# Attention on one core: rests of the turned weights in one bank for two groups, value products over 128 rows and then over 64

## The chip, the cores and the metric

The kernel runs on one core of one Trainium2 chip. The metric is the device time of one execution in microseconds; before the change the median of three runs is 2397.38 (2395.8 to 2399.34).

## The reference, cut to what matters

The reference is a trunk of two layers over 1024 tokens with 1024 features. Layer 0 mixes with a short convolution and a recurrence, layer 1 with sliding-window attention; each is followed by a squared-ReLU MLP. The change touches the attention alone:

```
scores = einsum("bcqkgd,bcskd->bckgqs", q, k_band) * HEAD_DIM ** -0.5   # 64-token chunks
scores = where(valid, scores + bias, NEG_INF)          # own chunk and the one before: band of 128 keys
m = maximum(max(scores), sink)
p = exp(scores - m)
denom = sum(p) + exp(sink - m)
o = einsum("bckgqs,bcskd->bcqkgd", p / denom, v_band)  # 16 query heads, 2 key/value heads, head_dim 64
y = o @ w_o
```

## The kernel before, in words

The attention works on eight tiles of 128 queries. The 16 heads of a tile go in four groups of four; groups 0 and 1 belong to the first key/value head, 2 and 3 to the second. A tile of 128 queries sees a window of WIN = 192 keys, so the weights of a group are 128 x 768 numbers. V is token-major in `VTOK`, nine blocks of 128 keys offset by 64 (`v_transposes`, `v_tokens_dve`); GpSimd copies the two blocks of a tile to `VST` (`v_tile`).

The loop is a software pipeline written out by hand (`attention`, and one function per engine: `round_pe`, `round_dve`, `round_act`, `round_pool`). A round works on the scores of tile `new` and on the values of tile `old = new - 1`. Six of the rounds (new = 2 to 7) have both; four of these are in a hardware loop. Each engine runs its queue in order and waits on semaphores; a `Track` numbers the steps of a tile.

- TensorE: per group g, `score_products` of group g + 1 (two fp32 products of 384 columns; the last of the round is group 0 of the next tile), then `probs_transposes` of group g of the old tile: four transposes of 128 x 128 into bank 4 (the block "a", the first 128 keys), four of 128 x 64 into the lower rows of bank 5 (the "rest", the last 64 keys). Groups 1 to 3 wait until both copies of the group before have emptied the banks. Behind group 3 come the `value_products`.
- VectorE: per group the biases (four operations), the maximum, the negation (`scores_dve`). Behind group 0 also the reciprocal of the old tile's denominators and the scaling of its group 0. It copies the rests out of bank 5 into `PTB` (`rest_copy`), one copy per group.
- ScalarE: per group four exponentials with their sums, then the copy of block "a" out of bank 4 into `PTA`. At the end of the round it copies the outputs of banks 6 and 7 into `Q`.
- GpSimd: scales the weights of groups 1 to 3 of the old tile, copies queries and V blocks.

`value_products` makes eight products: for each key/value head (bank 6, bank 7) one over `PTA` and one over `PTB`, each for even and odd heads (`par`), which go to the lower and upper 64 rows of the bank. All have 128 contracted rows and 512 columns. `PTB` holds only 64 rows of weights; its other 64 are set to zero once (`ptb_zero`) and contracted with what V has there. An fp32 product stands in the trace as two records.

## Time and profile before

| | |
|---|---|
| median of the runs, us | 2397.38 |
| profiled execution, its own time, us | 2398.16 |
| its span, us | 2396.4 |
| granted clock of TensorE, mean | 0.992 |
| TensorE busy, us | 2322.3 |
| VectorE busy, us | 1440.1 |
| ScalarE busy, us | 795.2 |
| GpSimd busy, us | 411.2 |
| attention, first value product to the end of the last, us | 1523.66 to 1635.95 |

The profiled execution is one run; its span is the time between the first and the last instruction, and the rest of its own time lies around it. Rows of the trace give a start in us from the span's start, a length, and the line of the kernel. PE is TensorE's products, PEld its weight loads, DVE VectorE, ACT ScalarE, POOL GpSimd.

### The profile page before, as it was taken

The page shows a single profiled execution, that of the slowest core. Times are in us where ns is not written, and L with a number is a line of the kernel's source. Part 1 is how long each engine was busy: PE and PEld are TensorE (multiplying, and loading weights), DVE is VectorE, ACT ScalarE, POOL GpSimd, SP SyncE. Part 2 cuts the span into 40 slices and gives each one's busy share as a digit, 9 for nine tenths or more (in the row PEclk, how much of TensorE's full clock was granted, in tenths as well). Part 3 has the DMA queues.
Part 4 walks back from the last instruction along what each step waited for, and adds up shares of the span by engine and source line. Part 5 has one row for each costly group of instructions (what it writes and reads, how often), then busy time and mean ns, then how long its engine had stood idle before and what let it go on. Part 6 is the DMA issues. An engine that isn't in the chain of part 4 may idle for free.

```text
span 2396.4 us, 41386 instructions
## 1 busy us (share of the span) xinstructions
PE 2322.3 (97%) x16368; PEld 1897.3 (79%) x16368; DVE 1440.1 (60%) x1994; ACT 795.2 (33%) x1265; POOL 411.2 (17%) x401
## 2 busy tenths in 40 slices
PE   7999999999999999999999999788999999999999
PEld 6888877787788888888888788446888888888887
DVE  4444567776347656655765823873465576567655
ACT  5111235444233322332333422563243233323323
POOL 0000011121232111211111400432321111111110
PEclk9999989999999999999999999999999999999999
DMA  3231100002111121111111110001111111121113
GB/s 127 71 140 58 45 11 4 3 3 100 53 43 55 44 62 53 44 53 53 53 50 54 48 53 27 1 0 40 40 53 53 53 53 44 52 61 44 53 53 88
DMA packets 167185, 119.30 MB, mean 50 GB/s; under 512 B 3662, under 2 KB 164260, under 8 KB 166564
## 3 DMA queue, kind: packets, MB, share of 16 engines
q1 hardware_dynamic: 164284, 100.65, 14.2%
q0 software_dynamic: 2736, 17.04, 1.9%
q8 instruction: 86, 1.41, 0.3%
q14 instruction: 23, 0.19, 0.0%
q10 hardware_dynamic: 56, 0.01, 0.0%
HBM read 106.68 MB, written 10.49 MB: 49 GB/s over the span
## 4 chain that ended last, share of the span: by engine, by line
PE 93%; DVE 4%; issue 1%; ACT 1%; DMA 0%; SPq 0%; DVEq 0%; ACTq 0%
PE ps L280 35%; PE ps L404 25%; PE ps L397 15%; PE ps L1189 2%; PE ps L1211 1%; PE ps L1962 1%; PE ps L2314 1%; DVE probs L1991 1%; PE ps L296 1%; PE ps L351 1%; DVE softmax_stats L1996 1%; PE ps L1248 1%; PE ps L1931 1%; PE ps L1726 1%; PE ps L1387 1%
## 5 line engine op out<-in xcount | busy, mean ns | idle before, releaser
L235 ACT CAST w_hi<-w_raw 128x1024 fp32r<-128x1024 f32 x180 | 189.3, 1052 | 813.6 <-PE ps L280 594.1
L764 DVE TENSOR_TENSOR residual<-residual,ps 128x512 f32<-128x512 f32 x448 | 299.6, 686 | 159.6 <-PE ps L404 155.8
L280 PE MATMUL ps<-h_hi,w_hi 128*128 128x512 f32 x1232 | 383.1, 392 | 4.8 <-DVE h_lo L647 3.7
L280 PE MATMUL ps<-h_lo,w_hi 128*128 128x512 f32 x1232 | 379.9, 389 | 0.0
L280 PE MATMUL ps<-h_hi,w_lo 128*128 128x512 f32 x1232 | 379.3, 389 | 0.0
L280 PEld LDWEIGHTS ps<-h_hi,w_hi 128*128 128x128 f32 x1232 | 229.2, 188 | 52.9 <-issue 4.5
L280 PEld LDWEIGHTS ps<-h_hi,w_lo 128*128 128x128 f32 x1232 | 231.3, 188 | 48.6
L280 PEld LDWEIGHTS ps<-h_lo,w_hi 128*128 128x128 f32 x1232 | 231.3, 188 | 48.6
L239 DVE TENSOR_TENSOR w_lo<-w_raw,w_hi 128x1024 fp32r<-128x1024 f32 x180 | 224.6, 1248 | 26.8 <-ACT w_hi L235 26.8
L732 POOL TENSOR_TENSOR w_sums_raw<-w_raw 128x256 f32<-128x256 f32 x64 | 52.0, 813 | 1067.3 <-DMA w_raw<-in_mlp_down 647.6
L397 PE MATMUL ps<-h_hi,w_hi 128*128 128x512 f32 x512 | 199.2, 389 | 0.0
L397 PE MATMUL ps<-h_lo,w_hi 128*128 128x512 f32 x512 | 199.2, 389 | 0.0
L397 PE MATMUL ps<-h_hi,w_lo 128*128 128x512 f32 x512 | 199.2, 389 | 0.0
L746 DVE SCALAR_TENSOR_TENSOR stage<-ps,rms_inverse 128x1024 f32<-128x1024 f32 x32 | 39.2, 1225 | 212.5 <-PE ps L280 212.5
L404 PE MATMUL ps<-t_hi,w_sums_hi 128*128 128x512 f32 x384 | 149.7, 390 | 0.0
L404 PE MATMUL ps<-t_hi,w_sums_lo 128*128 128x512 f32 x384 | 149.4, 389 | 0.0
L404 PE MATMUL ps<-t_lo,w_sums_hi 128*128 128x512 f32 x384 | 149.4, 389 | 0.0
L665 ACT CAST w_sums_hi<-w_sums_raw 128x1024 fp32r<-128x1024 f32 x64 | 67.2, 1049 | 227.9 <-POOL w_sums_raw L738 227.9
L397 PEld LDWEIGHTS ps<-h_lo,w_hi 128*128 128x128 f32 x512 | 96.1, 188 | 19.9
L397 PEld LDWEIGHTS ps<-h_hi,w_lo 128*128 128x128 f32 x512 | 96.1, 188 | 19.9
L397 PEld LDWEIGHTS ps<-h_hi,w_hi 128*128 128x128 f32 x512 | 96.1, 188 | 19.9
L642 DVE TENSOR_TENSOR stage<-ps,rms_inverse 128x1024 f32<-128x1024 f32 x30 | 36.7, 1225 | 110.3 <-PE ps L280 98.2
(389 smaller groups left out, 4012.9 us busy)
## 6 DMA issues: line engine op xcount, KB each, us to landing
w_raw<-in_mlp_up SPq DMA_DIRECT2D x64, 512.0 KB, 4.1
w_raw<-in_mlp_down SPq DMA_DIRECT2D x64, 512.0 KB, 3.4
w_raw<-in_w_in_ab SPq DMA_DIRECT2D x26, 512.0 KB, 3.8
w_raw<-in_w_qkv SPq DMA_DIRECT2D x10, 512.0 KB, 3.9
x_in_tile<-in_x POOLq DMA_DIRECT2D x8, 512.0 KB, 7.3
x_spill<-residual POOLq DMA_DIRECT2D x1, 4096.0 KB, 12.6
w_raw<-in_w_out_ab SPq DMA_DIRECT2D x8, 512.0 KB, 3.9
w_raw<-in_w_o SPq DMA_DIRECT2D x8, 512.0 KB, 3.9
```

What stands on the lines that cost most here:

```text
L235: nc.scalar.copy(WH[:, slot], WR[:, slot]).then_inc(w_hi, 1)
L239: nc.vector.tensor_tensor(WL[:, slot], WR[:, slot], WH[:, slot].bitcast(F32), ALU.subtract).then_inc(w_lo, 1)
L280: m = nc.tensor.matmul(acc(a_slot, half), ww, xx[:, k, half * HALF:(half + 1) * HALF], start=first, stop=last)
L296: m = nc.tensor.matmul(acc(1, half), ww, xx[:, k, half * HALF:(half + 1) * HALF], start=first, stop=last)
L397: m = nc.tensor.matmul(acc(slot, half), ww, xx[:, k, half * HALF:(half + 1) * HALF], start=first, stop=last)
L404: m = nc.tensor.matmul(PS[:, bank_n, :], ww[:, c], xx[:, c], start=new and c == 0 and ww is wh and xx is bh, stop=c == 1 and ww is wl, ski ...
L642: nc.vector.tensor_tensor(dst, acc2(slot), RI[:, :], ALU.mult).then_inc(acc_free[slot], 1)
L665: nc.scalar.copy(WSH[:, d % 2], WSR[:, d % 2]).then_inc(s_hi, 1)
L732: TT(raw[:, 0], a21, a22, ALU.add).then_inc(w_sum, 1)
L746: return nc.vector.scalar_tensor_tensor(dst, src, 0.0, scale, ALU.max, ALU.mult)
L764: dn_dve.done(TT(xk, xk, PS[:, bank_n, :], ALU.add), step)
L1189: m = MM(block_bank(bank_n, 32)[quarter(q), h], left[quarter(q), h], right[quarter(q), h], start=True, stop=True)
```

## The change

The nine offset blocks of V become eight plain ones, `VTOK` (the first 128 keys of each tile's window), and `VREST`, which holds for each tile the last 64 keys of the window twice, in the lower and in the upper 64 partitions. TensorE turns the latter with 16 operations of half width, ScalarE copies them (`v_rest_act`) before its first group of tile 1.

The weights' rests of groups 0 and 1 (and of 2 and 3) go into the lower and the upper rows of bank 5: the lower by a transpose, the upper by a true product with the identity (`turned`). ScalarE copies both at once into `PTB` ("r0", "r1"), behind the copy of the odd group's block "a". VectorE's rest copies go. Block "a" turns through banks 4, 6, 7 and 4 (`TA_BANK`).

`value_products` now goes by group: four pairs over 128 rows with 256 columns, the groups to banks 6, 7, 6, 7; then eight products over 64 rows (lower half of rows to bank 6, upper half to bank 7), 256 columns each. Only the first product of each bank and half of rows has `start`, and each of the last four products counts one step. ScalarE's output copies take the new order of heads in the banks. In the last round VectorE's split of the first output weights moves ahead.

```diff
--- before.py
+++ after.py
@@ -164,10 +164,11 @@
     SQ = at("squares", [S], 198.5)
     QST = at("q_tile", [2, KD, P], 32)
     VST = at("v_window", [2, 2, P], 43)
-    VTOK = at("v_token_major", [9, P], 190.5)
+    VTOK = at("v_token_major", [NT, P], 190.5)
+    VREST = at("v_rest_twice", [NT, P], 198.5)
     PP = at("probs", [2, NQ, WIN], 50)
     PTA = at("probs_t_a", [NQ, P], 74)
-    PTB = at("probs_t_b", [NQ, P], 82)
+    PTB = at("probs_t_b", [NKV, 4, P], 82)
     STA = at("softmax_stats", [2, 6, NQ], 195.25)
     QF = at("first_q_tile", [KD, P], 112)
     PF = (at("first_probs0", [4, WIN], 180.5), at("first_probs1", [4, WIN], 183.5), at("first_probs2", [4, WIN], 104))
@@ -1755,12 +1756,22 @@
 
             unit(9, 1, 4, {2: scores(0), 3: lambda: mean_square(8, 0), 4: scores(1), 6: spread_and_scores})
 
+        def turned(dst, src, half):
+
+            if half:
+                return nc.tensor.matmul(dst, src, ident, start=True, stop=True)
+            return nc.tensor.transpose(dst, src, ident)
+
         def v_transposes(t):
             t.wait_ge(acc_free[1], STAGE["qkv"][1] // 2 + 6)
             t.wait_ge(qk_norm, 2 + 9)
             sc_dve.wait(t, 0, "b3")
-            for n in range(9):
-                m = nc.tensor.transpose(bank((6, 7, 5)[n // 4])[:, n % 4], VP[:, P * n:P * n + P], ident)
+            for n in range(NT):
+                m = nc.tensor.transpose(bank(6 + n // 4)[:, n % 4], VP[:, P * n:P * n + P], ident)
+            m.then_inc(v_tr, 1)
+            for n in range(NT):
+                for half in two:
+                    m = turned(bank(4 + n // 4)[half_rows(half), n % 4], VP[:, P * n + P:P * n + P + RH], half)
             m.then_inc(v_tr, 1)
 
         def qkv_act(act):
@@ -1851,20 +1862,26 @@
 
         def v_tokens_dve(dve):
             dve.wait_ge(v_tr, 1)
-            for n in (0, 1, 2):
-                rows = 4 if n < 2 else 1
-                nc.vector.tensor_copy(VTOK[:, 4 * n:4 * n + rows], bank((6, 7, 5)[n])[:, 0:rows]).then_inc(v_tok, 1)
+            for n in two:
+                nc.vector.tensor_copy(VTOK[:, 4 * n:4 * n + 4], bank(6 + n)).then_inc(v_tok, 1)
+
+        v_rest = sem("v_rest_token_major")
+
+        def v_rest_act(act):
+            act.wait_ge(v_tr, 2)
+            for n in two:
+                nc.scalar.copy(VREST[:, 4 * n:4 * n + 4], bank(4 + n)).then_inc(v_rest, 1)
 
         q_pool = Track("q_tile_copied", ["q"])
-        v_pool = Track("v_tile_copied", ["v"])
+        v_pool = Track("v_tile_copied", ["own", "rest"])
         p_pool = Track("probs_pool", ["p1", "p2", "p3"])
         sc_pe = Track("score_pe", [f"sc{g}" for g in range(4)])
-        pv_pe = Track("value_pe", [f"t{w}{g}" for g in range(4) for w in "ab"] + ["pv"])
+        pv_pe = Track("value_pe", [f"t{w}{g}" for g in range(4) for w in "ab"] + ["pv0", "pv1", "pv2", "pv3"])
         sc_dve = Track("score_dve", [f"{w}{g}" for g in range(4) for w in ("b", "max", "neg")] + ["sink"])
-        pv_dve = Track("value_dve", ["den", "rcp", "p0", "e0", "e1", "e2", "e3"])
+        pv_dve = Track("value_dve", ["den", "rcp", "p0"])
         sc_act = Track("score_act", [f"e{g}" for g in range(4)] + ["sink"])
-        pv_act = Track("value_act", [f"e{g}" for g in range(4)] + ["o0", "o1"])
-        ptb_zero, nsnk_ok = sem("probs_rest_zero"), sem("minus_sinks_ready")
+        pv_act = Track("value_act", ["e0", "e1", "r0", "e2", "e3", "r1", "o0", "o1"])
+        nsnk_ok = sem("minus_sinks_ready")
         slopes = [2.0 ** (-8.0 * (h + 1) / NQ) for h in range(NQ)]
 
         def score_banks(tile, g):
@@ -1893,15 +1910,14 @@
             q_pool.done(nc.gpsimd.tensor_copy(QF[:, 6:8], Q[:, 6:8, 0:P]), "q")
             pool.wait_ge(acc_done, STAGE["qkv"][1] + 9 + 3)
             q_tile(pool, 1, 1)
-            q_pool.wait(pool, 1, "q")
-            nc.gpsimd.memset(PTB[RH:P], 0.0).then_inc(ptb_zero, 1)
-            pool.wait_ge(ptb_zero, 1)
 
         def v_tile(pool, tile, s):
             if not at_start(tile, 2):
-                pv_pe.wait(pool, tile - 2, "pv")
+                pv_pe.wait(pool, tile - 2, "pv3")
                 waited(pool, "pool")
-            v_pool.done(nc.gpsimd.tensor_copy(VST[:, s], VTOK[:, bass.ds(tile, 2), :]), "v")
+            for n, (v, step) in enumerate(((VTOK, "own"), (VREST, "rest"))):
+                v_pool.done(nc.gpsimd.tensor_copy(VST[:, s, n], v[:, bass.ds(tile, 1), :].rearrange("p a n -> p (a n)")),
+                            step)
 
         def score_products(t, tile, s, g):
             if at_start(tile, 1):
@@ -1932,36 +1948,48 @@
                                      K2[:, g // 2, :, bass.ds(tile * P, WIN)], start=True, stop=True)
             sc_pe.done(m, f"sc{g}")
 
+        TA_BANK = (4, 6, 7, 4)
+
         def probs_transposes(t, tile, s, g):
             if g:
                 p_pool.wait(t, tile, f"p{g}")
             else:
-                pv_dve.wait(t, tile, f"p{g}")
-            if g > 0:
-                pv_act.wait(t, tile, f"e{g - 1}")
-                pv_dve.wait(t, tile, f"e{g - 1}")
+                pv_dve.wait(t, tile, "p0")
+            if g == 3:
+                pv_act.wait(t, tile, "e0")
+            elif at_start(tile, 1):
+                t.wait_ge(v_rest, 2)
+            else:
+                pv_act.wait(t, tile - 1, ("r1", "o0", "o1")[g])
+            if g == 2:
+                pv_act.wait(t, tile, "r0")
             for j in range(4):
-                m = nc.tensor.transpose(bank(4)[:, j], probs(tile, s, g)[:, j, 0:P], ident)
+                m = nc.tensor.transpose(bank(TA_BANK[g])[:, j], probs(tile, s, g)[:, j, 0:P], ident)
             pv_pe.done(m, f"ta{g}")
             for j in range(4):
-                m = nc.tensor.transpose(bank(5)[0:RH, j], probs(tile, s, g)[:, j, P:WIN], ident)
+                m = turned(bank(5)[half_rows(g % 2), j], probs(tile, s, g)[:, j, P:WIN], g % 2)
             pv_pe.done(m, f"tb{g}")
 
         def value_products(t, tile, s):
-            pv_act.wait(t, tile, "e3")
-            pv_dve.wait(t, tile, "e3")
-            v_pool.wait(t, tile, "v")
-            if at_start(tile, 1):
-                t.wait_ge(ptb_zero, 1)
-            else:
-                pv_act.wait(t, tile - 1, "o1")
+            v_pool.wait(t, tile, "rest")
+
+            def out_of(g, par):
+                return PS[half_rows(par), 6 + g % 2].rearrange("p (k a m) -> p k a m", k=NKV, m=P)[:, g // 2]
+
+            for g in range(4):
+                pv_act.wait(t, tile, ("e1", "e2", "e2", "r1")[g])
+                for par in two:
+                    nc.tensor.matmul(out_of(g, par), VST[:, s, 0, RH * (g // 2):RH * (g // 2) + RH],
+                                     PTA[:, 4 * g + par:4 * g + 4:2], start=g < 2, stop=False, skip_group_check=True)
             for kv in range(NKV):
-                for n, pt in enumerate((PTA, PTB)):
-                    for par in two:
-                        o = PS[RH * par:RH * par + RH, 6 + kv].rearrange("p (a m) -> p a m", m=P)
-                        m = nc.tensor.matmul(o, VST[:, s, n, RH * kv:RH * kv + RH], pt[:, 8 * kv + par:8 * kv + 8:2],
-                                             start=n == 0, stop=n == 1)
-            pv_pe.done(m, "pv")
+                for par in two:
+                    for half in two:
+                        m = nc.tensor.matmul(out_of(2 * kv + half, par),
+                                             VST[half_rows(half), s, 1, RH * kv:RH * kv + RH],
+                                             PTB[half_rows(half), kv, par:4:2],
+                                             start=False, stop=True, skip_group_check=True)
+                        if kv:
+                            pv_pe.done(m, f"pv{2 * par + half}")
 
         def round_pe(t, new, old, s):
 
@@ -2023,30 +2051,21 @@
                         pv_dve.wait(dve, old, "den")
                         pv_dve.done(nc.vector.reciprocal(STA[:, o, 4], STA[:, o, 4]), "rcp")
                         pv_dve.wait(dve, old, "rcp")
-                    else:
-                        rest_copy(dve, old, g - 1)
-                        if new is None and g == 3:
-                            split_lo(dve, 0, STAGE["wo"][0])
                     if g == 0:
                         pr = probs(old, o, 0)
                         pv_dve.done(nc.vector.tensor_tensor(
                             pr, pr, STA[:, o, 4, hs].unsqueeze(2).to_broadcast([P, 4, WIN]),
                             ALU.mult), f"p{g}")
+                        if new is None:
+                            split_lo(dve, 0, STAGE["wo"][0])
             if new is not None:
                 sc_dve.wait(dve, new, "neg3")
                 sc_dve.done(nc.vector.tensor_tensor(STA[:, s, 3], SNK[:, :], STA[:, s, 2], ALU.add), "sink")
-            if old is not None:
-                rest_copy(dve, old, 3)
-
-        def rest_copy(dve, tile, g):
-            pv_pe.wait(dve, tile, f"tb{g}")
-            if g == 0 and not at_start(tile, 1):
-                pv_pe.wait(dve, tile - 1, "pv")
-            pv_dve.done(nc.vector.tensor_copy(PTB[0:RH, 4 * g:4 * g + 4], bank(5)[0:RH]), f"e{g}")
-
         def round_act(act, new, old, s):
             if new is None:
                 split_hi(act, 0, STAGE["wo"][0] // 2, STAGE["wo"][1] + 1)
+            if at_start(old, 1):
+                v_rest_act(act)
             for g in range(4):
                 if new is not None:
                     sc_dve.wait(act, new, f"neg{g}")
@@ -2060,12 +2079,17 @@
                         sc_act.done(nc.scalar.activation(STA[:, s, 5], STA[:, s, 3], ACT.Exp), "sink")
                 if old is not None:
                     pv_pe.wait(act, old, f"ta{g}")
-                    pv_act.done(nc.scalar.copy(PTA[:, 4 * g:4 * g + 4], bank(4)), f"e{g}")
+                    pv_act.done(nc.scalar.copy(PTA[:, 4 * g:4 * g + 4], bank(TA_BANK[g])), f"e{g}")
+                    if g % 2:
+                        pv_pe.wait(act, old, f"tb{g}")
+                        pv_act.done(nc.scalar.copy(PTB[:, g // 2], bank(5)), f"r{g // 2}")
             if old is not None:
-                pv_pe.wait(act, old, "pv")
-                waited(act, "act")
-                for kv in range(NKV):
-                    pv_act.done(nc.scalar.copy(Q[:, 4 * kv:4 * kv + 4, bass.ds(old * P, P)], bank(6 + kv)), f"o{kv}")
+                for half in two:
+                    pv_pe.wait(act, old, "pv3")
+                    waited(act, "act")
+                    pv_act.done(nc.scalar.copy(
+                        Q[:, :, bass.ds(old * P, P)].rearrange("p (k h a) m -> p h k a m", k=NKV, h=2)[:, half],
+                        bank(6 + half).rearrange("p (k a) m -> p k a m", k=NKV)), f"o{half}")
 
         def round_pool(pool, new, old, s):
             o = 1 - s
@@ -2082,9 +2106,9 @@
                         pr, pr, STA[:, o, 4, hs].unsqueeze(2).to_broadcast([P, 4, WIN]),
                         ALU.mult), f"p{g}")
             if at_start(old, 1):
-                pool.wait_ge(v_tok, 3)
+                pool.wait_ge(v_tok, 2)
+                pool.wait_ge(v_rest, 2)
                 v_tile(pool, 0, 0)
-                v_pool.wait(pool, 0, "v")
             if new is not None:
                 v_tile(pool, new, s)
```

## Rows read from the trace of the kernel before

**Rows 1.** The page: busy time by engine, and the chain by engine.

```profile
PE 2322.3 (97%) x16368; PEld 1897.3 (79%) x16368; DVE 1440.1 (60%) x1994; ACT 795.2 (33%) x1265; POOL 411.2 (17%) x401
...
PE 93%; DVE 4%; issue 1%; ACT 1%; DMA 0%; SPq 0%; DVEq 0%; ACTq 0%
```

**Rows 2.** Windows: us, busy us (instructions) by engine, granted clock, DMA share, GB/s.

```profile
1509.30:1511.80 2.50, 2.44 (x4) 0.78 (x3) 2.40 (x8) 1.86 (x8) 0.12 (x1) 0.56 0.00 0
...
1511.80:1514.00 2.20, 1.35 (x10) 1.22 (x11) 2.17 (x6) 0.59 (x1) 2.20 (x2) 1.00 0.00 0
...
1556.00:1572.20 16.20, 13.17 (x64) 7.20 (x64) 12.81 (x33) 10.40 (x39) 6.47 (x5) 1.00 0.00 1
```

**Rows 3.** Chain that ended last, in one round: start, us, what.

```profile
1555.73 0.30 issue
...
1556.03 3.66 PE ps L1962 x16
...
1559.68 1.50 PE ps L1931 x4
...
1571.24 0.69 DVE probs_t_b L2045
```

**Rows 4.** Timeline of one round: start, us, engine, line, operation, count [idle before <- releaser].

```profile
1558.48 5.09 POOL L2081 TENSOR_TENSOR probs<-probs,softmax_stats 128x768 f32<-128x768 f32 x3 [6.60 <-DVE softmax_stats L2024]
...
1559.61 1.56 PE L1931 MATMUL ps<-k_zero_padded,q_tile 128*128 x4
...
1559.89 1.07 ACT L2068 COPY q_then_o<-ps 128x512 f32 x2 [4.18 <-PE ps L1962]
...
1561.01 0.60 PE L1944 MATMUL ps<-constants,probs 128*128 128x128 f32 x4
...
1561.30 1.15 DVE L1991 SCALAR_TENSOR_TENSOR probs<-constants,ps 128x192 f32<-128x192 f32 x4 [1.91 <-PE ps L1931]
...
1561.88 1.46 PE L1931 MATMUL ps<-k_zero_padded,q_tile 128*128 x4
...
1563.66 0.45 ACT L2055 ACTIVATE probs<-probs,softmax_stats 128x192 f32<-128x192 f32 x1 [0.48 <-DVE softmax_stats L1999]
...
1564.40 0.66 PE L1944 MATMUL ps<-constants,probs 128*128 128x128 f32 x4 [1.06 <-DVE probs_t_b L2045]
...
1565.43 0.56 ACT L2063 COPY probs_t_a<-ps 128x512 f32<-128x512 f32 x1
...
1571.24 0.20 ACT L2060 ACTIVATE softmax_stats<-softmax_stats 128x16 f32<-128x16 f32 x1
...
1571.35 0.56 ACT L2063 COPY probs_t_a<-ps 128x512 f32<-128x512 f32 x1
```

**Rows 5.** Timeline: first round, and the value products of tiles 0, 6, 7.

```profile
1507.57 1.71 PE L1763 MATMUL ps<-constants,v_padded 128*128 128x128 f32 x9 [2.69 <-DVE v_padded L642]
...
1512.51 1.14 DVE L1991 SCALAR_TENSOR_TENSOR probs<-constants,ps 128x192 f32<-128x192 f32 x4
...
1523.66 1.08 PE L1962 MATMUL ps<-probs_t_a,v_window 128*64 128x512 f32 x4 [0.82 <-ACT probs_t_a L2063]
...
1620.15 1.08 PE L1962 MATMUL ps<-probs_t_a,v_window 128*64 128x512 f32 x4 [0.82 <-ACT probs_t_a L2063]
...
1624.89 1.06 ACT L235 CAST w_hi<-w_raw 128x1024 fp32r<-128x1024 f32 x1
...
1632.28 1.08 PE L1962 MATMUL ps<-probs_t_a,v_window 128*64 128x512 f32 x4 [0.82 <-ACT probs_t_a L2063]
```

**Rows 6.** Timeline of TensorE in the recurrent stage: tile shapes.

```profile
401.43 1.13 PE L1211 MATMUL ps<-a_r_b_k_dec 64*128 64x256 f32 x8
...
417.71 1.16 PE L1398 MATMUL ps<-gate_in,lora_w 128*128 128x128 f32 x8
...
418.80 1.14 PE L1404 MATMUL ps<-tri_inv_t,half_y 64*64 64x64 f32 x16
...
419.87 0.76 PE L1236 MATMUL ps<-a_r_b_k_dec 64*32 64x32 f32 x64
```

## The prediction

> **What bounds the kernel now.** I read the page first. TensorE is busy 97% of the span and makes up 93% of the chain that ended last [rows 1]; only where TensorE waits can a change to the attention pay. The windows then give the attention's stage: in a round of 16.2 us the engines are busy 13.2 (TensorE), 12.8 (VectorE), 10.4 (ScalarE) and 6.5 us (GpSimd), at a granted clock of 1.00 [rows 2]. No engine is full, so the round is set by a ring of waits, and I read the chain and the timeline of one round for it.
>
> The value products' 16 matmul records take 3.66 us, the next scores 1.50, and the last copy of rests on VectorE 0.69 with 0.30 us of issue behind it [rows 3]. VectorE stands still for 1.91 us before the biases of group 1: these need scores that are queued on TensorE behind the value products [rows 4]. TensorE then waits for VectorE's copies of rests (1.06 us at 1564.40), since all groups turn through banks 4 and 5 [rows 4]. So the ring is: last rest copy, value products, scores, VectorE's softmax work with four rest copies in it, last rest copy. Value products start at 1523.66 for tile 0 and 1620.15 for tile 6 [rows 5]: six rounds of 16.08 us. The last interval is 12.13 us.
>
> **The change, part by part.** Durations are those of the profiled execution (span 2396.4, its own time 2398.16, against a median of 2397.38 over the runs shown).
>
> *VectorE.* Four rest copies of 0.69 us leave each round: 12.8 becomes 10.1 us of work.
>
> *ScalarE.* Two copies of rests (128x512 from one bank) join. The nearest row is its copy of the same shape, 0.57 us [rows 4]; the output's strided copy, 1.07 us for two [rows 4], is about as dear, so the bounds are 0.54 and 0.60 and I take 0.57. 10.4 becomes 11.5 us. The output copies are cut by bank in another way, with as many elements: nothing.
>
> *TensorE, turning.* Groups 1 and 3 have their rests turned by a true product into the upper rows. Eight fp32 records of 128 columns took 1.09 us (417.71 to 418.80 in the recurrent stage, at line 1398), some 0.2 of it the tail before another tile shape [rows 6]; a group of four products is eight such records, so about 0.86 us, where four transposes took 0.44 (with the transposes of the blocks 0.87 from 1561.01 to 1561.88). Bounds 0.44 and 1.09; plus 0.42 twice a tile.
>
> *TensorE, values.* Before, 16 records of 512 columns took 3.58 us from the start to the next scores [rows 3, 4]: one record alone is 0.43 us (512 columns in two passes of 2.4 GHz), so two ran at a time, one in each half of columns. Now the own blocks need 16 records of 256 columns, two at a time: 16 x 0.215 / 2 = 1.72 us. The rests need 16 records of 256 columns in tiles of 64x64. Both kinds of overlap stand in the trace: 64-row products in two row halves, 8 records of 256 columns in 1.13 us with the tail, instead of 1.71 alone; and 64x32 tiles, 64 records in 0.76 us, where one after the other they would be 64 x 0.027 = 1.7 (32 columns in two passes) [rows 6]. Four at a time gives 16 x 0.215 / 4 = 0.86 us; I add 0.12 for the change of tile shape, as the scores after the value products had (1.40, where four records of 384 columns in two passes are 1.28). Bounds: 0.86 (four at once) and 3.44 (none at once; the 64x64 row at 418.80 shows 16 records of 64 columns in a single tile, 1.07 us, so alone they do queue) [rows 6]. I take 0.98 with the switch, since the 64x32 row is the nearest. The values then take 2.70 instead of 3.58 us.
>
> The Trainium skill (TensorEngine Tiling, Key Properties) says that a change of tiling mode drains the engine; the rows agree with some 0.1 to 0.2 us. Against the change speaks the skill's page TensorE: Matmul & The Clock Gate (The cost: per-tile semaphore tail): each further increment on a packed group costs some 26 ns. Four increments stand where one stood; by that page an estimate of 0.08 us per tile, 0.6 us in all. No row here shows it, and the sum leaves it out.
>
> *The order.* The first three groups of values no longer wait for the last copies: they run while ScalarE copies group 3 and the second pair of rests. Only the last own group (0.43) and the rests (0.98) stand behind the last copy.
>
> *The new round*, from the end of the last rest copy: issue 0.30; last own group 0.43; rests 0.98; scores of group 1 to VectorE's start 1.69 (1559.61 to 1561.30); biases, maxima and negation to the first exponential 2.36 (1561.30 to 1563.66); four exponentials 1.77 (1563.66 to 1565.43); copy and rest copy 1.14; four exponentials 1.77; copy 0.57; four exponentials 1.77, the sink 0.11, copy and rest copy 1.14 [rows 4]. Sum 14.03 us. ScalarE takes VectorE's place in the ring: what was VectorE's share is late no more. The nearest rival to the ring is TensorE: from the scores of group 1, those of group 2 start 2.27 later, end 1.31 on, the turning of group 1 takes 0.45 + 0.86, so the scores of group 3 start at 4.9, VectorE at 6.6, and the exponentials of group 3 could start at 8.95; ScalarE reaches them at 1.69 + 2.36 + 1.77 + 1.14 + 1.77 + 0.57 = 9.30. The cover over the dearer turning is thus 0.35 us; what it costs beyond that is on the path. GpSimd's three products (5.09 us [rows 4]) start at the reciprocal and are done before the third group's exponentials: covered. The two window copies in place of one, and the memset that goes, lie in GpSimd's idle time (it is busy 6.5 of 16.2 us [rows 2]).
>
> Gain of six rounds: 6 x (16.08 - 14.03) = 12.3 us.
>
> *Last round.* No scores are left; before, each group waited for both copies of the one before, 12.13 us. Now groups turn through banks 4, 6, 7, 4. From the last rest copy of tile 6: rest of its values 1.7, output copies 1.1 and 0.2 of latency, weight copy 1.06 [rows 5], two copies and a rest copy 1.7, turning of groups 2 and 3 with its latency 2.4, the last rest copy 0.9: 9.1 us. Gain 3.0. Behind it, the values' end: before 0.30 + 3.66, now 0.30 + 1.41: gain 2.2.
>
> *First round.* The value columns' turning grows from 9 transposes to 8 transposes and 16 of half width, of which eight are products: at full clock 8 x 0.11 + 8 x 0.22 = 2.6 us more. It falls where the granted clock is 0.56 (1509.3 to 1511.8), since TensorE had stood still for 2.69 us before 1507.57 [rows 2, 5]; from 1511.8 on it is 1.00, the level of 2.4 GHz [rows 2]. I place the end of it at 1512.8, the scores at 1514.1, and VectorE's biases at 1514.3 instead of 1512.51 [rows 5]. The path from there, by the terms above, is 2.36 + 2.91 + 2.34 + 3.02 = 10.6, so the last rest copy ends at 1524.9, where the copies before ended by 1523.5: 1.5 us lost. Bounds: a gain of 0.5 (if the pairs of half width overlap) and a loss of 4 (if the low clock lasts through the scores). ScalarE's two copies of the rests fall into its idle time.
>
> Sum: -12.3 - 3.0 - 2.2 + 1.5 = -16.0 us. The profiled time would be 2382.2 and the median 2381.4 us.
>
> **The rivals.** *Rests two at a time* (the row halves or the column halves, not both): 1.72 instead of 0.86 in six rounds, the last round and the end: + 8 x 0.86 = 6.9 us, so 2388.3. For it: no row shows 64x64 tiles in all four quarters; against it the 64x32 row.
>
> *Turning or ScalarE's copies dearer than their rows*, so that the cover of 0.35 is used up, or the low clock lasts in the first round: 0.3 to 0.6 us a round, 2384 to 2386.
>
> *No change*: a record of 256 columns in these tiles takes the 0.43 us of the wider one, because weight loads, one per record, don't hide. Own blocks 3.44, rests 1.72: from the start of values 5.28 instead of 3.2 us, so a round of 14.03 + 2.1 = 16.1, as before. Against it: the 64-row products of 256 columns above.
>
> *Slower*: the tiles don't overlap at all, the shorter records filling no second tile before the next wait. Own blocks 3.44 and rests 3.44 are 6.9 us from the start of values; a round is 14.03 + 3.7 = 17.7, six lose 10, the first 1.5, and the end loses 2 x 3.7 - 5.2 = 2.2: 2411. It decides from 5.2 us of values per tile on. Against it stands that the trace has pairs overlapping everywhere.
>
> **How the numbers follow.** Forecast 0.68; rests two at a time 0.14; dearer copies, turning or clock 0.08; no change 0.05; slower 0.05. The likeliest: 2381.4, its own range 2378 to 2384. The range to hold eight in ten takes in the first two rivals: 2378 to 2389. A measurement of this kernel can tell about 0.2%, 4.8 us: faster by more 0.90, within it 0.05, slower 0.05.
>
> **What would show it.** In the trace after: value products of a tile in 2.7 us with the rest products in under 1.1; four turning products in 0.86; intervals between tiles of 14.0 us; VectorE waiting again and ScalarE the engine of the chain, busy 11.5 us of a round; the scores after the value columns' turning near 1513. Wrong would be: rest products of 1.7 us or more; a wait of ScalarE for VectorE's negation of group 3 (then TensorE or VectorE is in the ring, not ScalarE); a granted clock under 1.00 behind the first round.

## The result and the profile after

The kernel after takes 2380.74 us (median of four runs, 2377.6 to 2382.13), the kernel before beside it 2398.36 (2395.8 to 2407.29); the ratio is 0.9913, 95% interval 0.9895 to 0.9931. The median is 0.7 us off the forecast, the direction is right, and this time is in the range. But the two medians are 17.6 us apart, and the ratio, which sets runs beside each other, says 20.9 us gained (16.5 to 25.2), where the forecast had 16.0. Counted from 2397.38 that is 2376.5 us, below the range's 2378: the gain was sized too small. The profiled execution took 2380.53 us, its span is 2378.6.

The page after: busy time by engine, and the chain that ended last by engine, beside [rows 1].

```profile
PE 2326.3 (98%) x16583; PEld 1909.8 (80%) x16583; DVE 1420.9 (60%) x1961; ACT 802.9 (34%) x1283; POOL 411.9 (17%) x408
...
PE 94%; DVE 3%; ACT 1%; issue 1%; DMA 0%; SPq 0%; ACTq 0%; DVEq 0%
```

TensorE has 4 us more to do and the span is 17.8 us shorter, so what went is waiting. The windows after (columns as in [rows 2]): the stretch that had a clock of 0.56 before, one round of the loop, and the start of the output product.

```profile
1509.30:1511.80 2.50, 2.50 (x13) 1.39 (x13) 1.27 (x3) 0.24 (x1) 2.07 (x1) 1.00 0.00 0
1554.00:1568.00 14.00, 13.67 (x92) 9.03 (x91) 10.57 (x29) 11.53 (x44) 7.21 (x7) 1.00 0.00 0
1620.00:1624.00 4.00, 3.70 (x9) 2.97 (x10) 4.00 (x5) 4.00 (x5) 0.00 (x0) 0.57 0.02 4
```

VectorE and ScalarE are near the forecast's 10.1 and 11.5 us a round (10.57 and 11.53 in a window of 14.0, slightly longer than a round), but TensorE is busy 13.67 of 14.0 where it had been 13.17 of 16.2 [rows 2]. The reader should take a first warning here: an engine at 98% of a round is a candidate for its bound.

One round of the timeline after, from the last own block of one tile (columns as in [rows 4]; an "own block" is the product of a group over its first 128 keys). L2082 copies a block "a", L2085 a pair of rests, L2074 is the exponential, L2019 the biases, L2027 the negation of the maximum:

```profile
1564.07 0.58 ACT L2085 COPY probs_t_b<-ps 128x512 f32<-128x512 f32 x1
...
1564.69 0.20 PEld L1982 LDWEIGHTS ps<-probs_t_a,v_window 128*64 128x64 f32 x4 [0.54 <-ACT probs_t_b L2085]
...
1565.28 1.09 PE L1987 MATMUL ps<-probs_t_b,v_window 64*64 64x256 f32 x16
...
1566.30 1.56 PE L1947 MATMUL ps<-k_zero_padded,q_tile 128*128 x4
...
1567.99 1.15 DVE L2019 SCALAR_TENSOR_TENSOR probs<-constants,ps 128x192 f32<-128x192 f32 x4 [2.26 <-PE ps L1947]
...
1568.13 0.60 PE L1763 MATMUL ps<-constants,probs 128*64 128x128 f32 x4
...
1568.57 1.46 PE L1947 MATMUL ps<-k_zero_padded,q_tile 128*128 x4
...
1570.39 0.85 PEld L1762 LDWEIGHTS ps<-constants,probs 128*64 128x64 f32 x8 [0.17 <-issue]
1570.39 1.09 PE L1762 MATMUL ps<-constants,probs 128*64 128x128 f32 x8
1570.42 0.46 ACT L2074 ACTIVATE probs<-probs,softmax_stats 128x192 f32<-128x192 f32 x1 [0.45 <-DVE softmax_stats L2027]
...
1571.41 0.94 PEld L1947 LDWEIGHTS ps<-k_zero_padded,q_tile 128*128 128x128 f32 x4 [0.17 <-issue]
...
1572.19 0.56 ACT L2082 COPY probs_t_a<-ps 128x512 f32<-128x512 f32 x1
...
1572.66 0.58 ACT L2085 COPY probs_t_b<-ps 128x512 f32<-128x512 f32 x1
...
1573.09 1.15 DVE L2019 SCALAR_TENSOR_TENSOR probs<-constants,ps 128x192 f32<-128x192 f32 x4 [0.42 <-PE ps L1947]
1573.13 0.46 ACT L2074 ACTIVATE probs<-probs,softmax_stats 128x192 f32<-128x192 f32 x1
...
1573.29 0.66 PE L1967 MATMUL ps<-constants,probs 128*128 128x128 f32 x4 [0.32 <-ACT probs_t_b L2085]
...
1574.90 0.57 ACT L2082 COPY probs_t_a<-ps 128x512 f32<-128x512 f32 x1
...
1575.26 0.16 DVE L2027 SCALAR_TENSOR_TENSOR softmax_stats<-softmax_stats,minus_sinks 128x4 f32<-128x4 f32 x1
...
1575.46 0.46 ACT L2074 ACTIVATE probs<-probs,softmax_stats 128x192 f32<-128x192 f32 x1
```

The 16 rest records take 1.02 us to the next scores (1565.28 to 1566.30): four at a time. Four turned products take 1.02 (1570.39 to 1571.41), four transposes of the other group's rests 0.44 (1568.13 to 1568.57). Tile to tile, the rests start every 13.74, 13.73, 13.74, 13.73, 13.65 and 13.64 us; the last interval is 9.12.

By stage, in the two profiled executions. The stages are cut at four starts: the scores of tile 1's group 1 (1503.32 before, 1502.06 after), the first value product behind tile 0's last copy (1523.66, 1523.49), the same of tile 6, and the first output product (1639.61, 1620.30):

| us | before | after | difference | forecast |
|---|---|---|---|---|
| to tile 0's values behind the last copy | 20.34 | 21.43 | +1.1 | +1.5 |
| six rounds | 96.49 | 82.22 | -14.3 | -12.3 |
| last round and values' end | 19.46 | 14.59 | -4.9 | -5.2 |
| attention | 136.29 | 118.24 | -18.05 | -16.0 |
| ahead of it | 1503.32 | 1502.06 | -1.3 | 0 |
| behind it | 756.8 | 758.3 | +1.5 | 0 |

The 1.3 us ahead of the attention are less than two executions of one kernel differ by: a second trace of the kernel before (e9) comes to the same point at 1498.16, 5.2 us earlier.

### The profile page after: what moved, and what is told of

Same layout as the page of the kernel before. It is cut to its first block, busy times and chain, and to the rows that moved or that the text cites. A ratio compares the mean times of both kernels' runs of the same rounds, so it can differ in the third digit from the quotient of the medians.

```text
span 2378.6 us, 41798 instructions
## 1 busy us (share of the span) xinstructions
PE 2326.3 (98%) x16583; PEld 1909.8 (80%) x16583; DVE 1420.9 (60%) x1961; ACT 802.9 (34%) x1283; POOL 411.9 (17%) x408
## 4 chain that ended last, share of the span: by engine, by line
PE 94%; DVE 3%; ACT 1%; issue 1%; DMA 0%; SPq 0%; ACTq 0%; DVEq 0%
PE ps L281 35%; PE ps L405 25%; PE ps L398 15%; PE ps L1190 2%; PE ps L1212 1%; PE ps L1947 1%; PE ps L352 1%; PE ps L297 1%; PE ps L1249 1%; PE ps L2338 1%; PE ps L1727 1%; PE ps L1388 1%; PE ps L1221 1%; PE ps L1982 1%; ACT probs L2074 0%
```

## The experiments

"Round" is the distance between two tiles' rest products in the four tiles of the loop. Each run was compared with the kernel before on its own chip, in which that kernel's median was 2403 to 2406 us.

**e1: the kernel after again.**

> The changed kernel unaltered, timed beside the kernel before in five rounds. Two theories of the size: (A) the gain is what the two traces of the attention show (18.0 us between the first tile's last scores and the first output product) less 1.5 us of low clock behind it: 16.5 to 18 us, ratio 0.9925 to 0.9932. (B) the ratio of the first comparison (0.9913) is the size: 21 us, and something outside the attention gives 3 us. A says 2380 beside 2397.5, B says 2376.5.

2384.56 us, ratio 0.9916 (0.9893 to 0.9938). Rounds 13.74, 13.73, 13.74, 13.73, last 9.12, end as before: the ring repeats to 0.01 us. The first round took 26.28 us where it had taken 22.01, at this clock (window):

```profile
1506.00:1518.00 12.00, 11.98 (x43) 6.31 (x44) 5.19 (x14) 3.70 (x16) 6.09 (x7) 0.57 0.00 0
```

The 0.57 is mostly 0.50, the level of 1.2 GHz. So a low clock in the first round costs this kernel 4.3 us, and a third trace (e16) had it at 1502 to 1506 instead, for 1.5 us.

**e2: all value products wait for the second pair of rests.** Undoes the order alone.

```diff
         def value_products(t, tile, s):
             v_pool.wait(t, tile, "rest")
+            pv_act.wait(t, tile, "r1")
```

> The value products of all groups wait for ScalarE's last copy of rests (as they all waited for the last copy before the change). Theory (the ring runs over that copy, the first three groups' products lie beside ScalarE): 3 x 0.43 = 1.3 us more in each of seven rounds and 0.8 us at the last tile, so 9.8 us over the changed kernel, some 2390. Rival (the gain comes from VectorE alone, the order is worth nothing, TensorE has slack behind): within 2 us of the changed kernel.

2399.42 us, ratio 0.9975 (0.9955 to 0.9995); rounds 15.10. TensorE:

```profile
1570.82 1.95 PE L1983 MATMUL ps<-probs_t_a,v_window 128*64 128x256 f32 x16 [1.45 <-ACT probs_t_b L2086]
```

+1.37 us a round: the three groups' 1.29 us come whole onto the path. This is the largest single part of the gain that was isolated, 8 of the 14 us of the six rounds. The median is 14.9 us above e1's where 9.8 had been expected; at an equal clock (below) it is 11 us.

**e3: the rest products twice.** Their part of the output is doubled.

```diff
-            for kv in range(NKV):
+            for rep, kv in ((0, 0), (0, 1), (1, 0), (1, 1)):
...
-                        if kv:
+                        if kv and rep:
```

> The eight 64-row products of the rests are issued twice (their part of the output is doubled). Theory (four tiles at a time and on the path): 0.85 us more for each of eight tiles, 6.8 us over the changed kernel, some 2387.5; the rest products' rows 1.9 us instead of 1.02. Rival (two at a time): 1.7 us each, 13.7 us, 2394. Rival (hidden): under 1 us.

2388.19 us, ratio 0.9933 (0.9912 to 0.9955); rounds 14.60, last 9.99, end 5.73.

```profile
1568.00 1.96 PE L1987 MATMUL ps<-probs_t_b,v_window 64*64 64x256 f32 x32
```

Sixteen more records, 0.87 us more in every interval: 16 x 0.215 / 4 = 0.86. Four at a time, all of it on the path; the rival "two at a time" is out.

**e4: the second rest copy on VectorE**, behind the next tile's first biases.

```diff
...
+        def second_rest_dve(dve, tile):
+            pv_pe.wait(dve, tile, "tb3")
+            pv_dve.done(nc.vector.tensor_copy(PTB[:, 1], bank(5)), "r1")
...
-                    if g % 2:
+                    if g == 1:
```

TensorE's waits for that copy go to VectorE's semaphore.

> The second copy of rests (groups 2 and 3) goes back to VectorE, between the biases and the maximum of the next tile's group 0, where VectorE has 2 us of slack before its next wait. Theory (ScalarE is the engine of the ring): ScalarE's 0.48 us at the end of the round goes and the copy is done 0.35 us earlier, 2.5 us under the changed kernel over seven rounds, some 2378. Rival (TensorE, 13.67 of 14.0 us busy, is as good as the bound): no difference, within 1 us. Rival (VectorE's delay of the denominators reaches the transposes): slower by 0.3 us a round, 2382.

2389.24 us, ratio 0.9937 (0.9912 to 0.9962); rounds 14.14 and 14.11, longer by 0.4, where shorter was expected. The timeline:

```profile
1574.42 5.09 POOL L2119 TENSOR_TENSOR probs<-probs,softmax_stats 128x768 f32<-128x768 f32 x3 [5.76 <-DVE softmax_stats L2065]
...
1578.67 0.85 DVE L2037 SCALAR_TENSOR_TENSOR softmax_stats<-softmax_stats,minus_sinks 128x4 f32<-128x4 f32 x1
...
1579.56 0.45 ACT L2088 ACTIVATE probs<-probs,softmax_stats 128x192 f32<-128x192 f32 x1 [1.07 <-DVE softmax_stats L2037]
```

The copy delays VectorE's reciprocal and with it GpSimd's three products, which end at 1579.51. VectorE's negation of group 1, 0.16 us elsewhere, lasts until then. In the kernel after the products end at 1569.91 and the negation starts at 1570.15: a margin of 0.24 us that the forecast had called "covered" without pricing it. The forecast had also put GpSimd's window copies into its idle time; there the same negation lasts 0.23 us, until the second of them ends at 1570.38.

**e5: the four turned products of group 1 twice.**

```diff
+            for j in range(4 if g == 1 else 0):
+                m = turned(bank(5)[half_rows(g % 2), j], probs(tile, s, g)[:, j, P:WIN], g % 2)
```

> The four products that turn group 1's rests are issued twice. Theory (they lie between the scores of groups 2 and 3 with a cover of 0.35 us by the prediction, of 0.1 us by the trace): 0.87 us more for TensorE, 0.5 to 0.8 us more a round, so intervals of 14.2 to 14.5 us instead of 13.73, some 4 to 6 us in all. Rival (ScalarE's ring alone, the turning hidden): 13.7 us.

2389.41 us, ratio 0.9928 (0.9904 to 0.9952); rounds 14.61: +0.87.

```profile
1564.46 1.96 PE L1762 MATMUL ps<-constants,probs 128*64 128x128 f32 x16
```

Eight more records and 0.87 us more a round: nothing of them is covered. With a cover of 0.35 us it would have been 0.52. This is the run that puts TensorE's turning and the scores of group 3 in the ring, not ScalarE alone.

**e6: the own blocks of groups 0 to 2 twice.** The output counts them twice.

```diff
+                for par in two if g < 3 else ():
+                    nc.tensor.matmul(out_of(g, par), VST[:, s, 0, RH * (g // 2):RH * (g // 2) + RH],
+                                     PTA[:, 4 * g + par:4 * g + 4:2], start=False, stop=False, skip_group_check=True)
```

> The own-block products of groups 0 to 2 are issued twice (the output counts them twice). Theory (they lie beside ScalarE's last copies, and TensorE stands still for 0.32 to 0.54 us before the last own group): of 1.3 us more, 0.5 hidden, 0.8 on the path, intervals of 14.5 us, 6 us in all. Rival (fully hidden): 13.7 us; rival (no cover at all): 15.0 us.

2389.72 us, ratio 0.9932 (0.9911 to 0.9952); rounds 14.73: +1.0 of the 1.29 us added. Only 0.3 us of them found TensorE idle.

**e7: all four blocks "a" through bank 4.** Undoes the banks 6 and 7 alone; each group waits for ScalarE's copy of the one before, and the value products for the output copies.

```diff
-        TA_BANK = (4, 6, 7, 4)
+        TA_BANK = (4, 4, 4, 4)
...
-            if g == 3:
-                pv_act.wait(t, tile, "e0")
+            if g:
+                pv_act.wait(t, tile, f"e{g - 1}")
...
```

> The blocks 'a' of all groups are turned in bank 4 again, each group waiting for ScalarE's copy of the one before; the rest of the change stays. Theory (in the rounds the copies are done before TensorE comes to the next group, so the banks matter in the last round alone): intervals within 0.3 us of 13.73, and 1 us more in the last tile's round. Rival (the bank rotation is a main part of the gain): intervals over 14.5 us.

2381.62 us (two runs), ratio 0.9897 (0.9855 to 0.994); rounds 13.88 to 13.96, the last 13.44 where it was 9.12. The two runs don't tell it from the kernel after; the trace does: 0.2 us a round, and 4.3 us in the last round. But the last round of this trace fell into a low clock, 0.50 from 1609 to 1615, and the turning shows it: the first row stands in this trace, the second in the kernel after's.

```profile
1609.50 1.97 PE L1762 MATMUL ps<-constants,probs 128*64 128x128 f32 x8
```

```profile
1608.91 1.09 PE L1762 MATMUL ps<-constants,probs 128*64 128x128 f32 x8
```

Without the waits between them, the turnings of groups 1 to 3 take 6.45 us here and 3.57 there; so of the 4.3 us some 2.9 are the clock and, as an estimate, 1.4 the bank, near the 1 us that had been expected. The last round took 12.13 us before [rows 5] and takes 9.12 after: the banks are about half of that gain, and no run isolates the rest.

**e8: the next tile's scores of group 1 ahead of the last own block.**

```diff
+                if g == 3 and ahead:
+                    ahead()
                 pv_act.wait(t, tile, ("e1", "e2", "e2", "r1")[g])
...
-                if new is not None and g < 3:
+                if new is not None and g < 3 and (g or at_start(new, 2)):
...
-                value_products(t, old, 1 - s)
+                value_products(t, old, 1 - s, (lambda: score_products(t, new + 1, 1 - s, 1)) if ahead else None)
```

> The scores of the next tile's group 1 are issued ahead of the last own group instead of behind the rest products, while TensorE would wait for ScalarE's last copy. Theory (the ring is last copy, value products, scores, biases): VectorE's biases start 1.9 us earlier, the ring falls to about 12, and TensorE's own work (some 13.1 us) is the bound: intervals of 13.1 to 13.3 us, 3 to 4 us under the changed kernel. Rival (ScalarE's own sequence is the bound): 13.7 us.

2386.87 us, ratio 0.9933 (0.9909 to 0.9956); rounds 14.51 to 14.60: slower by 0.8, so taking the 1.6 us out of TensorE's part of the ring made another.

```profile
1566.57 1.09 PE L1989 MATMUL ps<-probs_t_b,v_window 64*64 64x256 f32 x16
...
1567.98 1.07 ACT L2093 COPY q_then_o<-ps 128x512 f32 x2 [3.54 <-PE ps L1989]
```

ScalarE stands still for 3.54 us before the output copies (2.03 in the kernel after), and the next tile's exponentials are queued behind them.

**e9: the kernel before again.**

> The kernel before, unaltered: what its attention takes in a second execution, and what two runs of one kernel differ by. From the scores of tile 1's group 1 to the first output product it took 136.3 us in the first trace, at a granted clock of 0.56 over 1509.3 to 1511.8. Theory A (the change's gain is all in the six rounds, the last one and the end): rounds 16.1 us again, the stage within 5 us of 136.3, and the ratio within 0.3% of 1. Rival B (the measured gain of some 20 us against 18 in the pair of traces is there because the kernel before loses more to low granted clock than the kernel after): stretches under 0.9 in this trace that the kernel after has not, and a stage above 136.3 by more than 2 us.

2402.31 us, ratio 1.0012 (0.9994 to 1.003). Rounds 16.24, 16.11, 16.21, 16.11; the attention 140.8 instead of 136.3, 0.8 us of it in the first round and 3.7 in the last, which fell into a low clock, as rival B of the expectation had it. The execution as a whole took 2397.53 us, no more than the first trace's 2398.16, since it came to the attention 5.2 us earlier. The low clock of the last round:

```profile
1624.00:1636.00 12.00, 9.54 (x32) 4.51 (x32) 2.50 (x3) 1.76 (x4) 0.00 (x0) 0.60 0.15 44
```

**e10: the kernel before with its four rest copies on ScalarE.** The change's relief of VectorE alone.

```diff
-                        rest_copy(dve, old, g - 1)
...
                     pv_act.done(nc.scalar.copy(PTA[:, 4 * g:4 * g + 4], bank(4)), f"e{g}")
+                    pv_pe.wait(act, old, f"tb{g}")
+                    pv_act.done(nc.scalar.copy(PTB[0:RH, 4 * g:4 * g + 4], bank(5)[0:RH]), f"f{g}")
...
```

> The kernel before, but ScalarE makes the four copies of rests, one per group and unpacked, in place of VectorE. One part of the change alone: VectorE's relief. Theory A (the ring holds the full value products and three groups of exponentials and copies on one engine): 0.30 + 3.58 + 1.69 + 2.43 + 3 x 1.77 + 3 x 2 x 0.47 + 0.11 = 16.2 us a round, as before (16.08), or 16.8 if a copy costs its recorded 0.57; the last round 1 to 2 us more than its 12.1: 2398 to 2405, within 0.3% of the kernel before. Rival B (taking the copies off VectorE is what brings the gain): 14 to 15 us a round, 8 to 12 us faster.

2406.35 us, ratio 1.0024 (1.0005 to 1.0042); rounds 16.11. One of 17.80 and the last of 14.08 fell into a clock of 0.50.

```profile
1554.21 1.08 PE L1960 MATMUL ps<-probs_t_a,v_window 128*64 128x512 f32 x4 [1.80 <-ACT probs_t_b L2054]
```

VectorE's copies taken away gain nothing while the whole value products stand behind the last copy and ScalarE has four unpacked copies to make in their place. A copy costs ScalarE 0.47 us from start to start here too, and with it the expectation's sum of 16.2 us a round came true. So neither "VectorE was the bottleneck" nor the copy's recorded length holds. e2 has the two packed copies without the new order: 15.10 us a round.

**e11: as e8, and ScalarE's output copies behind the next tile's group-0 exponentials.**

```diff
...
                 if old is not None:
+                    if g == 0 and not at_start(old, 1):
+                        outputs_act(act, old - 1)
                     pv_pe.wait(act, old, f"ta{g}")
...
```

> The kernel after with the scores of the next tile's group 1 ahead of the last own block and the rests, and with ScalarE's output copies behind the next tile's group-0 exponentials, where the run with the scores ahead alone had ScalarE stand for 3.5 us in front of the output copies. Theory A (that stand in an in-order queue was the reason of its loss): the output copies no longer hold up exponentials, the ring loses the last own block and the rests (1.6 us) and TensorE's own work of 13.2 to 13.5 us becomes the bound: 13.2 to 13.6 us a round instead of 13.73. Rival B (the ring runs through the last copy of rests and the bank it frees in either order): 13.7 us or more a round.

2383.17 us, ratio 0.9924 (0.9898 to 0.9951); rounds 13.27. The window of one:

```profile
1560.20:1573.47 13.27, 13.27 (x90) 8.78 (x89) 10.92 (x28) 11.28 (x42) 6.59 (x6) 1.00 0.00 0
```

TensorE is busy 13.27 of 13.27 us: here it is the bound itself. It confirms why e8 lost. The first round is 1.6 us longer at full clock (23.58), probably since the scores of tile 2 now stand ahead of tile 0's last block; the attention takes 115.76 us, 2.5 less than after.

**e12 and e13: the kernel after with TensorE's idle time filled**, ahead of the value columns and behind the last value product.

```diff
         def v_transposes(t):
+            t.wait_ge(qk_norm, 2 + 9)
+            for _ in range(3):
+                nc.tensor.matmul(PS[:, 7, 0:384], ident, CON[:, 0:384], start=True, stop=True)
             t.wait_ge(acc_free[1], STAGE["qkv"][1] // 2 + 6)
-            t.wait_ge(qk_norm, 2 + 9)
...
             attention(t, round_pe)
+            for _ in range(5):
+                nc.tensor.matmul(PS[:, 5, 0:384], ident, CON[:, 0:384], start=True, stop=True)
```

> The kernel after with fp32 products of 384 columns whose results nobody reads: three in TensorE's idle time before the value columns are turned (2.2 us), five between the last value product and the first output product. Theory A (the idle time is what the low granted clock follows, and that clock is what makes the first round 24.5 to 28 us in most traces instead of 22.0): the granted clock stays at 1.00 from 1506 to 1518, the first round takes 22.0 to 22.5, no low clock behind the end of the values, and the time is 2 to 6 us under the kernel after's. Rival B (the low clock comes in its own time, whatever TensorE does): granted clock under 0.8 somewhere in 1506 to 1518 again and a first round above 24; no gain.

> The kernel after with TensorE's idle time before the value columns and before the first output product filled with products whose results nobody reads, again, now beside the kernel before filled in the same way. Theory B (the clock favours the kernel after by 2 to 4 us over the forecast): this run and the filled kernel before differ by 16 to 18 us. Rival A (the clock costs both as much): by 20 us or more. By the last run the trace has 1.00 from 1506 to 1518, a first round of 22.0 us, rounds of 13.73.

2382.89 us, ratio 0.9923 (0.99 to 0.9946), and 2383.38, ratio 0.989 (0.9859 to 0.9921). Both traces have a clock of 1.00 throughout the attention, a first round of 22.02 and 22.03, and 756.7 and 756.8 us behind the attention instead of 758.3. The first output products, in the kernel after and then in e12:

```profile
1620.30 0.93 PE L281 MATMUL ps<-h_hi,w_hi 128*128 128x512 f32 x2 [3.78 <-DVE h_lo L648]
1621.03 1.06 PE L281 MATMUL ps<-h_lo,w_hi 128*128 128x512 f32 x2
1621.88 1.06 PE L281 MATMUL ps<-h_hi,w_lo 128*128 128x512 f32 x2
```

```profile
1618.69 0.70 PE L281 MATMUL ps<-h_hi,w_hi 128*128 128x512 f32 x2 [0.38 <-DVE h_lo L648]
1619.24 0.62 PE L281 MATMUL ps<-h_lo,w_hi 128*128 128x512 f32 x2
1619.70 0.62 PE L281 MATMUL ps<-h_hi,w_lo 128*128 128x512 f32 x2
```

In the traces the fill works; in the medians it can't be seen (e16, unfilled, took 2379.08 on the same chip as e13).

**e14: the kernel before with the same fill.**

> The kernel before with the same products in the same two places. Its first round was 20.3 and 21.1 us in two traces with a granted clock of 0.53 to 0.62 and 0.50 to 0.79 in it; filled I expect 1.00 there and 20.0 us. The low clock of the last round (0.50 from 1624 to 1634 in one trace, values' end 4.3 us later) lies between waits for copies that stay empty, so it may come again. Theory B: 2 to 4 us faster than the kernel before, ratio 0.9985. Rival A: ratio 1.000.

2400.87 us, ratio 0.9969 (0.9946 to 0.9992): 4 us faster than the kernel before by the medians, 7 by the ratio. Its trace still has the low clock twice: 0.50 in 1512 to 1514, behind a wait of 2.59 us for the first weights, and here:

```profile
1624.00:1636.00 12.00, 7.74 (x36) 4.83 (x36) 3.86 (x5) 3.96 (x7) 1.37 (x1) 0.65 0.15 45
```

**e15 and e16: all three edits (e11 and e12 together), and the kernel after once more.**

> The kernel after with the next tile's scores of group 1 ahead, ScalarE's output copies behind the next group-0 exponentials, and the idle time filled: rounds of 13.27 (13.73 less 0.46), first round 22.0, last round 8.65, so 3 us under the filled kernel after and some 3 to 6 under the kernel after: 2376 to 2380 beside a kernel before of 2400, ratio 0.990. Rival: the filled products move the start of the value columns or the scores ahead make the first round longer (23.58 in the run with both moves), and nothing is gained over the filled kernel.

> The kernel after unaltered on the same chip as the three others: rounds 13.73, ratio 0.991 to 0.992, 3 to 6 us above the version with all three edits if their gains of the traces reach the time, 0 if not.

2378.75 us, ratio 0.9868 (0.9837 to 0.9898), against 2379.08, ratio 0.9878 (0.9847 to 0.991). e15's trace has rounds of 13.27, the attention in 115.74 us and 756.8 behind it, 4 us less than a trace of the kernel after; the intervals overlap all the same, so that it beats the kernel after is not shown.

**Where the rest of the measured gain is.** Each run lists its mean granted clock. Over 94 runs of the kernel before it is 0.9896 on average, over 16 of the kernel after 0.9923, and in each kernel the time falls with it. One slope for all kernels together is 2.03 us for 0.001. Set to a clock of 0.992 by that slope, the kernel before takes 2399.8 us (its mean's error 0.2) and the kernel after 2382.6 (0.4): 17.2 us, as the pair of profiled executions has it (17.6). The mean clocks' 0.0027, at 2.03 us for 0.001, are another 5.5 us between the two kernels' runs. The filled kernel before is at 0.9924 where the unfilled one beside it was at 0.9886; the filled kernel after gains on it 17.5 us by the medians, 16.8 at an equal clock and 19.0 by the two ratios.

At an equal clock the experiments fall into place too. Against the kernel after, e2 costs 11.1 us, e3 6.3, e4 2.6, e5 5.7, e6 7.8 and e8 6.0, with errors of 0.5 to 1.0; e11 and e15 gain 1.3 and 1.6, with errors of 1.1 and 0.8. e10 takes what the kernel before takes, 2399.8.

Most of the low clock does not lie in the attention. Cut the trace into stretches of 2 us, take for each one minus its granted clock, times its length, and add them up: ahead of the attention the kernel before has 17.0 us of it in its first trace and 6.8 in e9, the kernel after 13.6, 11.9 and 9.2 in its three. In the attention it is 1.7 and 6.8 before, 0.7, 5.1 and 2.4 after; behind it 1.4 and 1.4 before, 3.9, 4.4 and 4.3 after. Stages that both kernels share thus lose 10 us more or less from one execution to the next of the same kernel, and with four runs on each side part of the ratio can be that draw.

## Why the prediction was right, and where it was not

Three steps failed, one of them in the mechanism. *The new round* was summed too long, 14.03 for 13.74 us, since ScalarE's five copies in it stood at their recorded length of 0.57 instead of the 0.47 from start to start. *"ScalarE takes VectorE's place in the ring"* failed, since the cover of 0.35 us was -0.05 and the ring runs through TensorE as well. And the sum put *the granted clock outside the first round* at nothing, without a reason: 17.2 us of the gain are there at an equal clock, and the other 3.7 of the ratio's 20.9 go with the clock of the runs. The new round accounts for 1.7 us of the miss. Why the clock is higher in the runs of the kernel after stays open. That the median came within 0.7 us of the forecast is in part luck: beside the kernel before on two other chips the same kernel gained 19.5 us (e1) and 26.0 (e16) by the medians.

*What bounds the kernel, the ring of waits*: right. e10 shows it best: with VectorE relieved and the ring otherwise left as it was, a round stays at 16.11 us.

*Rests four at a time, own blocks two at a time*: right (1.02 against 0.98 us; e3: 0.87 for 16 more; in e2 the 16 own records take 1.87 us to the rests, 1.72 and a change of shape). *The order*: right (e2: 1.37 us). By the Trainium skill (TensorEngine Tiling, Key Properties) a change of tiling mode drains the engine. The trace agrees around true products: 0.17 us of "issue" before the weight loads at 1570.39 and 1571.41, 0.39 before those of the rests and of the scores behind them, and 0.16 us each in the 1.02 us of the turned products and of the rests. Around the transposes, whose rows carry the same shape 128*64, it shows nothing: 0.44 us at 1568.13, and the scores follow at once. The 0.08 us a tile that I had worked out from the Trainium skill's page TensorE: Matmul & The Clock Gate (The cost: per-tile semaphore tail) can't be told apart in any run here.

*The new round* is the term that was mis-sized, 14.03 against 13.74 us. Step by step after 1564.69: last own block 0.59 (0.43 forecast), rests 1.02 (0.98), to VectorE 1.69, to the exponential 2.43 (2.36; GpSimd's window copy lengthens the negation by 0.07), four exponentials 1.77, copy and rest copy 0.94 (1.14), four exponentials 1.77, copy and a wait of 0.09 0.56 (0.57), and exponentials, sink, copy, rest copy and wait 2.97 (3.32 with the issue). The copies' recorded 0.56 to 0.58 us overlap the next instruction's start: from start to start they take 0.47. Five of them are in these terms, and I had read the length, not the distance.

*ScalarE takes VectorE's place in the ring; the cover over the dearer turning is 0.35 us*: this step failed. ScalarE would have reached group 3 at 1574.90 + 0.47 = 1575.37, 9.07 us behind the scores of group 1 (9.30 forecast), and VectorE's negation ended at 1575.42, 9.12 behind them (8.95 forecast; the turning of group 1 took 0.53 and 1.02 where 0.45 and 0.86 stood, the two changes of shape). The cover is -0.05: two paths of one length, and the ring runs through TensorE. e5 shows it, 0.87 us for 0.87 added. A third path comes close: TensorE waits 0.32 us for the first rest copy (1573.29) and has no recorded wait from there to the last own block at 1578.43; e6, 1.0 us for 1.29 added, leaves it 0.3 us to spare. Both ends of the cover had been a few tenths off in opposite directions, which is as much as it was. The forecast's own sign of it, ScalarE waiting for the negation of group 3, is in the trace: 0.09 us, 1575.37 to 1575.46.

*Six rounds*: -14.3 instead of -12.3, of which 6 x 0.29 = 1.7 are the term above; 0.2 are the fifth and the sixth round's 13.65 and 13.64. *Last round and end*: -4.9 against -5.2, right; by e7 the banks bring about half of the last round's 3 us. *First round*: +1.1 in the pair of traces, at full clock, against +1.5; e1 had +5.4 at a clock of 0.57, beyond the bound of 4. The forecast placed the low clock from one trace, and its place moves from run to run. *Behind the attention*: the forecast had nothing; three traces of the kernel after have a low clock in the first output products and 758.3 us behind them, two traces of the kernel before 756.8 and 756.7. +1.5 us.

*The rivals.* The rests run four at a time, and e3 excludes "two at a time". The second rival came true in its conditions, for the turning was dearer than its row, the cover was used up, and e1 had the low clock; but the copies were cheaper, and the round was shorter, not longer. "No change" and "slower" set their value products against 3.2 us, where the sum had 2.70; nothing in the prediction explains the 3.2, and with 2.70 both would have come out 0.5 us a round longer.

*The measured ratio* lies outside the forecast by more than the attention's terms, which come to 2 us; 3.7 go with a mean clock that is higher in the runs of the kernel after. The forecast had no term for the clock outside the first round. That the waits in the kernel before bring the lower clock is argued only: filling two idle stretches raised it (e14), but the trace of that run still had low stretches elsewhere, and no trace was taken of a run at 0.987, the level at which the kernel before often is. The traces that there are, at 0.991 to 0.994, show in sum as much low clock in the one kernel as in the other. Open is also which of its waits does it.

## What to carry to other kernels

When an engine's share is taken out of a ring of waits, sum every path round the ring again, from start to start of the instructions, and call two paths that differ by less than the rows' own overlap equal: the next bound is then either. Taking work off the engine that seems last gains nothing if a long step stays behind it (e10), and moving a step forward in one queue pays only once what is queued behind its consumer has moved too (e8 against e11). Before reading a step's length from one trace, look at the granted clock in it (e7's last round). Where a gain is of the size of the clock's spread, take several traces of both kernels and compare stages, or compare runs at equal granted clock.

## What the runs showed of the hardware that was not expected

- VectorE's negation, 0.16 us by itself, lasts until GpSimd's product ends if it starts while one is in progress: 0.85 us in e4, 0.34 to 0.69 in e11. VectorE's biases, which read scores from a bank, keep their 1.15 us beside the same product (e4, 1576.51).
- ScalarE's copy of 128x512 from a bank is recorded at 0.56 to 0.58 us and takes 0.47 from start to start.
- The granted clock falls to 0.50, the level of 1.2 GHz, in some executions of a kernel and not in others. Most falls came behind waits of TensorE of 2.2 to 3.8 us (first round, output product); in e9's last round it came among waits of 0.9 to 1.7 us, and in one round of e10's loop behind one of 1.8. The first round of one kernel took 22.0 or 26.3 us by that alone.
- A change between products in tiles of 128x128, 128x64 and 64x64 costs 0.1 to 0.16 us; transposes in rows of 128*64 between rows of 128*128 cost nothing (0.44 us at 1568.13).
